# Paged decode: the product of probabilities and latents dealt to four 32-column strips of TensorE

## The chip, the cores and the metric

One core of a Trainium2 chip runs the whole program. The metric is the device time of one execution in microseconds, from the first to the last instruction; it is measured several times, and the median counts.

## What is computed

One inference step of a two-layer trunk. Each layer normalises its input, projects it once to all branch columns, runs a retention branch and a latent-attention branch for 512 prompt tokens and for 8 sequences with 8 new tokens each, and projects back. The change touches only the attention of those 8 sequences over their paged past:

```python
def one(xs):                       # one decode sequence
    pt, qn_s, qp_s, c_s, kpe_s = xs
    c_all = concatenate([cache_ckv[layer, pt].reshape(-1, KV_RANK), c_s])    # 16 pages x 128 rows, and 8 new
    kp_all = concatenate([cache_kpe[layer, pt].reshape(-1, MLA_ROPE), kpe_s])
    kn, v = mla_keys_values(c_all[None], p)          # kn = rmsnorm(c @ w_kb), v = c @ w_vb
    ...
    s = einsum(qn, kn) + einsum(qp, kp_all)
    pr = softmax(where(mask, s * MLA_SCALE, NEG_INF))
    return einsum('bhqk,bkhd->bqhd', pr, v)
```

The kernel never makes v. It computes (pr @ c_all) @ w_vb: the latents (256 wide) are weighted by the probabilities first, and one small product per head follows for all sequences together. All is float32.

## The kernel before, in words

The program is written by hand for five engines with semaphores between them; each engine runs its own list of instructions in the order in which the code stands. A loop of two layers has five stages with a meeting point between them (`stage_end`): the input projection, the latents and prompt keys, retention and prompt attention, the paged decode, and the output projection. The projections are made in three products of rounded high and low parts. The change is in the fourth stage.

In the decode stage the unit is a pair of pages. A sequence has 8 pairs (`PAIRS`), and a layer has 8 sequences. For each pair TensorE turns the next pair's latents (`turn_pair`, L838) and rotary keys (L843), multiplies the turned latents by the key weights with the sequence's queries beside them (`pair_keys`, L861), and multiplies the rotary part (`pair_rotary`, L870). ScalarE keeps the turned latents' high part (L1178), squares the keys (L1191) and keeps the scores (L1194, L1196). VectorE makes the low part (L1547) and sums the squares (L1564), GpSimd takes the inverse root (L1803 to L1810), and VectorE joins the scores (L1573, L1578).

The rest of a sequence, its tail, is spread over the pairs of the next sequence. The functions `sequence` of each engine set the place by the pair's number q: the maximum is turned behind pair 1 (`tail_max_turn`, L878) and spread behind pair 2 (L882), ScalarE takes the exponential behind pair 3 (L1201), and then TensorE does the three steps that the change touches:

- `tail_attend` behind pair 4 (L890): for each of the 16 pages, and for the new rows (`c_new`, 64 rows), the probabilities (128 rows of keys by HQ = 32 columns, 4 heads times 8 queries) are the weights and the page's 256 latents move. All 17 add up in partitions 0 to 31 of one part of PSUM bank 7. After every fourth page a semaphore (`pv_ps`) lets SyncE load four pages of a later sequence into that buffer.
- `tail_den` behind pair 5 (L898): the denominators, which VectorE has summed per partition (L1602), are summed over partitions by a product with one column of ones.
- VectorE divides (`tail_divide`, L1607 and L1609), and `tail_turn` behind pair 6 (L905) turns the 32 x 256 result into two 128 x 32 pieces with a product by the identity. VectorE keeps them (L1616).

The last sequence of a layer has no next one; its tail runs alone at the end of the stage, each step waiting for the last. The closing products with w_vb follow (L946).

```python
                for n in range(KT):
                    ...
                    m = pe.matmul(ps[0:HQ, 7, O_PV:O_PV + KVR], Pr[0:r, b, n, :], rhs,
                                  start=n == 0, stop=n == KT - 1)
```

Page latents and rotary keys come by one DMA each per page, issued by SyncE (L447, L449) after it has read the page number. A table of constants is loaded once at the start (L386).

Of the kernel before, what the change touches and what calls it, by code (L numbers as in the profile page):

```python
# [23 lines left out]
FP32 = mybir.dt.float32  # L24
# [5 lines left out]
P = 128  # L30
# [4 lines left out]
ROPE, QR, KVR = 64, 384, 256  # L35
# [22 lines left out]
QPAGES = NPAGE // QUARTERS  # L58
KT = NPAGE + 1
HQ = H * NT  # L60
LOG_G = np.log1p(-np.exp2(-5.0 - np.arange(H, dtype=np.float32))).astype(np.float32)


def rows(t):
    return ST if t == S_TILE else P
# [3 lines left out]
def constants():  # L69
    f = np.float32  # L70
    p = np.arange(P)
    pos = np.stack([p + P * t for t in range(TILES - 1)] + [NPAGE * PAGE + p % NT], 1).astype(f)

    def rope(dim):
        inv = (f(10000.0) ** (-(np.arange(0, dim, 2, dtype=f) / f(dim)))).astype(f)
        ang = (pos[:, :, None] * inv).astype(f)
        return np.cos(ang).astype(f), np.sin(ang).astype(f)

    cr, sr = rope(DK)
    ca, sa = rope(ROPE)  # L80

    place = np.stack([p, p % NT], 1).astype(np.float64) + 1.0
    g = LOG_G.astype(np.float64)
    dq = np.exp(place[:, :, None] * g)
    dk = np.exp(-place[:, :, None] * g) * DK ** -0.5
    decay = np.concatenate([dq, dk], 2)
    chunk_decay = np.broadcast_to(np.exp(P * g)[None, :], (P, H))
    causal = p[:, None] <= p[None, :]
    future = np.where(p[None, :] <= p[:, None], 0.0, NEG)
    s = np.arange(ST)  # L90
    same = s[:, None] // NT == s[None, :] // NT
    step_mask = np.zeros((P, ST))
    step_mask[:ST] = same & (s[:, None] <= s[None, :])
    new_mask = np.zeros((P, NB, H, NT))
    new_mask[:ST] = np.where(same & (s[:, None] <= s[None, :]), 0.0, NEG).reshape(ST, NB, 1, NT)
    own = np.zeros((P, NB))
    own[:ST] = s[:, None] // NT == np.arange(NB)[None, :]
    parts = [("ident", np.eye(P)), ("ones", np.ones((P, P))), ("causal", causal), ("future", future),
             ("step_mask", step_mask), ("new_mask", new_mask), ("own", own), ("cos_r", cr), ("sin_r", sr),
             ("cos_a", ca), ("sin_a", sa), ("decay", decay), ("chunk_decay", chunk_decay),  # L100
             ("neg_half", np.full((P, 1), -0.5)), ("key_mean", np.tile([[1.0 / DK, EPS]], (P, 1)))]
    at, place_of, cols = 0, {}, []
    for name, a in parts:
        a = np.asarray(a, np.float64).reshape(P, -1).astype(f)
        place_of[name] = (at, a.shape[1])
        cols.append(a)
        at += a.shape[1]
    return np.ascontiguousarray(np.concatenate(cols, 1)), place_of


CONST, PLACE = constants()


def build(nc, x_prompt, x_sample, cache_ckv, cache_kpe, state_ret, page_table, norm_w, w_in, q_a_norm_w,
# [5 lines left out]
    def place(name, shape, dt=FP32, at=base):  # L120
        n = 4 * int(np.prod(shape[1:]))
        tensor = nc.alloc_sbuf_tensor_at(name, shape, dt, offset=at[0])
        at[0] += (n + 31) // 32 * 32
        return tensor
# [4 lines left out]
    def const_view(name):  # L129
        a, n = PLACE[name]  # L130
        return cst[:, a:a + n]

    ident, ones, neg_half = const_view("ident"), const_view("ones"), const_view("neg_half")
    norm_b = place("norm_b", [P, D])
    gn_b = place("gn_b", [P, HW])
    qa_b = place("qa_b", [P, QR])
# [7 lines left out]

    wq_hi = place("wq_hi", [P, KC, HQ + HW + HQ], FP32R)
    wq_lo = place("wq_lo", [P, KC, HQ + HW + HQ], FP32R)
    wvb = place("wvb", [P, KC, HW])
    pages = place("pages", [1, NB * NPAGE], INT32)
    stat = place("stat", [P, 64])
    rstat = place("rstat", [P, 64])  # L150
    pool_tmp = place("pool_tmp", [P, 64])
    A0 = base[0]

    at = [A0]
# [8 lines left out]
    at = [A0]  # L163
# [29 lines left out]
    at = [E0]  # L193
# [26 lines left out]
    at = [D0]  # L220
# [8 lines left out]
    cT_lo = place("cT_lo", [P, 2, 2 * KC, P], FP32R, at)  # L229
    ksq = place("ksq", [P, 2, 2, HQ + HW], FP32, at)  # L230
    kss = place("kss", [P, 2, HALF, H], FP32, at)
    kss_t = place("kss_t", [P, 2, 2, H], FP32, at)
    krs = place("krs", [P, 2, HALF, H], FP32, at)
    nope = place("nope", [P, 2, NPAGE, HQ], FP32, at)
    rot = place("rot", [P, 2, NPAGE, HQ], FP32, at)
    Pr = place("Pr", [P, 2, KT, HQ], FP32, at)
    m1 = place("m1", [P, HQ], FP32, at)
    m2 = place("m2", [HQ, 1], FP32, at)
    mdiag = place("mdiag", [HQ, HQ], FP32, at)
    den = place("den", [P, HQ], FP32, at)  # L240
    rden = place("rden", [HQ, 1], FP32, at)
    on_s = place("on_s", [HQ, KVR], FP32, at)

    N0 = OG[1] - OG[0]
    at[0] = max(at[0], W_HI1)
# [7 lines left out]
    ps = nc.alloc_psum_tensor("ps", [P, 8, 512], FP32)  # L253
# [4 lines left out]
    def sem(name, per_layer=True):  # L258
        s = nc.alloc_semaphore(name)
        if per_layer:  # L260
            layer_sems.append(s)
        return s
# [6 lines left out]
    def mix_tile(k):  # L269
# [45 lines left out]
    den_ok, den_ps, pv_ps, pv_all, on_ok, ot_ps, pv_ok = (sem(n) for n in  # L315
        ("denominators_summed", "denominators_turned", "latents_attended_a_quarter", "latents_attended", "latents_divided",
         "attended_turned", "attended_kept"))
# [207 lines left out]
    def _(pe):  # L525
# [29 lines left out]
        with pe.Fori(0, DEPTH) as L:  # L555
# [36 lines left out]
            for h in range(H):  # L592
                for c in range(KC):
                    n = h * KC + c
                    m = pe.transpose(ps[:, 6 + n // 4, (n % 4) * P:(n % 4 + 1) * P], wkb[:, c, h * DK:(h + 1) * DK],
                                     ident)
# [78 lines left out]
            for c in range(KC):  # L675
                for h in range(H):
                    n = c * H + h
                    m = pe.matmul(ps[:, 0, n * ST:(n + 1) * ST], wkbT[:, h, c * P:(c + 1) * P],
                                  qnT[:, h, SEQ:TOK], start=True, stop=True)
# [194 lines left out]
            O_MT, O_MB, O_PV, O_DEN, O_T = 0, P, P + HQ, P + HQ + KVR, P + HQ + KVR + 1  # L874
# [10 lines left out]
            def tail_attend(s, b):  # L885
                pe.wait_ge(pr_ok, s + 1)
                for n in range(KT):
                    r = ST if n == NPAGE else P
                    rhs = c_new[0:r, :] if n == NPAGE else ckv[b][:, n, :]
                    m = pe.matmul(ps[0:HQ, 7, O_PV:O_PV + KVR], Pr[0:r, b, n, :], rhs,  # L890
                                  start=n == 0, stop=n == KT - 1)
                    if n % QPAGES == QPAGES - 1:
                        m.then_inc(pv_ps, 1)
                m.then_inc(pv_all, 1)

            def tail_den(s):
                pe.wait_ge(den_ok, s + 1)
                pe.matmul(ps[0:HQ, 7, O_DEN:O_DEN + 1], den[:, :], ones[:, 0:1], start=True, stop=True)\  # L898
                    .then_inc(den_ps, 1)

            def tail_turn(s):
                pe.wait_ge(on_ok, s + 1)
                for c in range(KC):
                    o = P + HQ + KVR + 16 + c * HQ
                    m = pe.matmul(ps[:, 7, o:o + HQ], on_s[:, c * P:(c + 1) * P], ident[0:HQ, 0:HQ],  # L905
                                  start=True, stop=True)
                m.then_inc(ot_ps, 1)

            def sequence(seq, b, use, next_use, first, last):
# [27 lines left out]
            tail_max_turn(NB - 1)  # L937
            tail_max_spread(NB - 1)
            tail_attend(NB - 1, 1)
            tail_den(NB - 1)  # L940
            tail_turn(NB - 1)

            pe.wait_ge(pv_ok, NB)
            for h in range(H):
                for c in range(KC):
                    m = pe.matmul(ps[0:ST, 0, h * DK:(h + 1) * DK], olat[:, c, h, :], wvb[:, c, h * DK:(h + 1) * DK],  # L946
                                  start=c == 0, stop=c == KC - 1)
# [30 lines left out]
    def _(act):  # L978
# [11 lines left out]
        with act.Fori(0, DEPTH) as L:  # L990
# [138 lines left out]
            def step_scale(h):  # L1129
                act.wait_ge(up_ok, h + 1)  # L1130
                act.activation(S0[:, h, :, :], S0[:, h, :, :], ACT.Copy, scale=float(np.exp(NT * np.float64(LOG_G[h]))))\
                    .then_inc(up_scaled, 1)
# [117 lines left out]
    def _(dve):  # L1250
# [17 lines left out]
        with dve.Fori(0, DEPTH) as L:  # L1268
# [335 lines left out]

            def tail_divide(s):
                dve.wait_ge(den_ps, s + 1)
                dve.reciprocal(rden[:, :], ps[0:HQ, 7, P + HQ + KVR:P + HQ + KVR + 1])  # L1607
                dve.drain()
                dve.tensor_scalar(on_s[:, :], ps[0:HQ, 7, P + HQ:P + HQ + KVR], rden[:, 0:1], None, ALU.mult)\  # L1609
                    .then_inc(on_ok, 1)  # L1610

            def tail_keep(s):
# [43 lines left out]
            tail_shift(NB - 1, 1)  # L1656
            tail_den(NB - 1, 1)
            tail_divide(NB - 1)
            tail_keep(NB - 1)
            dve.wait_ge(dy_ps, 1)  # L1660
# [20 lines left out]
            for g in range(3):  # L1681
# [3 lines left out]
                for t in range(TILES):  # L1685
                    n = rows(t)
# [161 lines left out]
```

## Time and profile before

| | |
|---|---|
| time, median of 3 runs | 1590.44 us (1587.83, 1592.5, 1590.44) |
| span of the profiled execution, on its one core | 1591.7 us, mean granted TensorE clock 0.936 |
| TensorE busy | 1450.8 us, 91% of the span, 8808 matmul records |
| VectorE, ScalarE, GpSimd busy | 727.7, 520.8, 423.9 us |
| matmul records of the attend (L890) | 544, of which 512 for pages |
| DMA | 115.82 MB, 24.2% of the time of 16 engines on the main queue |

The profiled execution is listed by its span alone, and no time of its own beside it; the span stands 1.3 us above the median of the runs. How to read it: times are microseconds unless marked ns. PE is TensorE's matmul, PEld its weight load, which overlaps PE, DVE VectorE, ACT ScalarE, POOL GpSimd, SP SyncE; a q behind the name is the engine's sequencer. L12 is line 12 of the kernel before. An fp32 product appears as two matmul records with a weight load each. Matmuls are pipelined and their ends are modelled, so the start of a record says more than its length. In the form 128\*32 the first number is the rows of the array that a product uses, the second its columns.

### The profile page before, as it was taken

To read this page: it belongs to the slowest core of one execution; us is meant where nothing else is said; L and a number is where in the kernel's file an instruction comes from. 1 tells how busy PE (TensorE), PEld (TensorE's weight loads), DVE (VectorE), ACT (ScalarE), POOL (GpSimd) and SP (SyncE) were. 2 spreads that over 40 slices of the span, in tenths; PEclk is the share of its full clock that TensorE was granted. 3 is DMA by queue.
4 is the path that set the end of the run, shared out by engine and by line. 5 is a ranking of instruction groups with operands and counts; after the bars stand their busy time and mean duration, and the time that the engine had idled before them with its cause. 6 is when DMAs were issued, how large, how long until landed. Compare 5 with 4: busy or idle time off the path is not lost.

```text
span 1591.7 us, 27121 instructions
## 1 busy us (share of the span) xinstructions
PE 1450.8 (91%) x8808; PEld 1241.1 (78%) x8808; DVE 727.7 (46%) x1366; ACT 520.8 (33%) x1360; POOL 423.9 (27%) x588
## 2 busy tenths in 40 slices
PE   5999987988999999978969999879989999999788
PEld 5999944666988888867959999446569888888578
DVE  4432445375555544543244324463855555545341
ACT  4210234132544444422041112331235444444230
POOL 1000222252544444430010002222525444444200
PEclk9999998588999999988979999975989999999899
DMA  9412020012442222201513210200135222222024
GB/s 307 132 53 74 0 72 0 1 40 70 129 117 67 66 67 66 67 1 59 180 65 127 65 61 0 72 0 1 41 83 165 68 67 66 67 66 67 1 92 166
DMA packets 132774, 115.82 MB, mean 73 GB/s; under 512 B 46513, under 2 KB 127346, under 8 KB 132658
## 3 DMA queue, kind: packets, MB, share of 16 engines
q1 hardware_dynamic: 132658, 114.49, 24.2%
q8 instruction: 46, 0.75, 0.2%
q14 instruction: 70, 0.57, 0.1%
HBM read 103.53 MB, written 13.27 MB: 73 GB/s over the span
## 4 chain that ended last, share of the span: by engine, by line
PE 43%; issue 31%; POOL 14%; POOLq 5%; DVE 4%; ACT 2%; DVEq 1%; DMA 0%; SPq 0%; ACTq 0%
POOL krs L1810 12%; PE ps L529 10%; PE ps L530 10%; PE ps L531 10%; POOL rstat L1703 2%; POOLq L1804 2%; POOLq L1806 2%; PE ps L725 2%; PE ps L890 1%; PE ps L772 1%; PE ps L770 1%; PE ps L543 1%; POOLq L1698 1%; PE ps L735 1%; PE ps L753 1%
## 5 line engine op out<-in xcount | busy, mean ns | idle before, releaser
L529 PE MATMUL ps<-w_hi,hT_hi 128*128 128x408 f32 (+5 forms) x880 | 304.2, 346 | 0.0
L530 PE MATMUL ps<-w_lo,hT_hi 128*128 128x408 f32 (+5 forms) x880 | 302.1, 343 | 0.0
L531 PE MATMUL ps<-w_hi,hT_lo 128*128 128x408 f32 (+5 forms) x880 | 301.2, 342 | 0.0
L1564 DVE TENSOR_REDUCE kss<-ksq 128x8 f32<-128x1024 f32 x128 | 156.0, 1218 | 232.1 <-ACT ksq L1191 232.1
L1191 ACT ACTIVATE ksq<-ps 128x544 f32<-128x544 f32 x256 | 160.0, 625 | 203.3 <-PE ps L861 203.3
L861 PE MATMUL ps<-wq_hi,cT_hi 128*128 128x272 f32 x1024 | 224.5, 301 | 0.0
L1810 POOL TENSOR_TENSOR krs<-kss_t,cst 128x8 f32<-128x8 f32 x128 | 209.1, 1634 | 19.0 <-DVE Ssc L1578 2.5
L861 PE MATMUL ps<-wq_lo,cT_hi 128*128 128x272 f32 x1024 | 213.5, 290 | 0.0
L861 PE MATMUL ps<-wq_hi,cT_lo 128*128 128x272 f32 x1024 | 213.4, 290 | 0.0
L529 PEld LDWEIGHTS ps<-w_hi,hT_hi 128*128 128x128 f32 (+1 forms) x880 | 158.6, 180 | 7.8 <-issue 0.2
L530 PEld LDWEIGHTS ps<-w_lo,hT_hi 128*128 128x128 f32 (+1 forms) x880 | 158.5, 180 | 7.4
L531 PEld LDWEIGHTS ps<-w_hi,hT_lo 128*128 128x128 f32 (+1 forms) x880 | 158.3, 180 | 7.6
L861 PEld LDWEIGHTS ps<-wq_lo,cT_hi 128*128 128x128 f32 x1024 | 162.8, 190 | 0.0
L861 PEld LDWEIGHTS ps<-wq_hi,cT_lo 128*128 128x128 f32 x1024 | 162.7, 190 | 0.0
L861 PEld LDWEIGHTS ps<-wq_hi,cT_hi 128*128 128x128 f32 x1024 | 161.3, 191 | 0.1
L1697 POOL TENSOR_SCALAR pool_tmp<-stat 128x1 f32<-128x1 f32 (+2 forms) x70 | 18.3, 261 | 491.4 <-ACT ps L1025 296.7
L1291 DVE TENSOR_SCALAR z<-ps 128x408 f32 (+3 forms) x80 | 45.7, 579 | 205.9 <-PE ps L531 205.7
L1178 ACT ACTIVATE cT_hi<-ps 128x512 fp32r<-128x512 f32 x128 | 77.6, 606 | 147.1 <-PE ps L838 146.0
L1547 DVE TENSOR_TENSOR cT_lo<-ps,cT_hi 128x512 fp32r<-128x512 f32 x128 | 87.3, 682 | 78.0 <-ACT cT_hi L1178 77.6
L890 PE MATMUL ps<-ckv,Pr 128*32 128x256 f32 x512 | 118.3, 391 | 3.0 <-ACT Pr L1201 3.0
L1803 POOL TENSOR_TENSOR kss_t<-kss,cst 128x8 f32<-128x8 f32 x128 | 29.0, 226 | 338.0 <-DVE kss L1564 338.0
L1005 ACT ACTIVATE w_hi<-raw 128x816 fp32r<-128x816 f32 x64 | 52.0, 877 | 202.8 <-PE ps L531 200.9
(181 smaller groups left out, 1948.1 us busy)
## 6 DMA issues: line engine op xcount, KB each, us to landing
ckv<-in_cache_ckv SPq DMA_DIRECT2D x256, 128.0 KB, 2.1
raw<-in_w_in SPq DMA_DIRECT2D x68, 408.0 KB, 4.4
kp<-in_cache_kpe SPq DMA_DIRECT2D x256, 32.0 KB, 1.8
raw<-in_w_out SPq DMA_DIRECT2D x16, 340.0 KB, 4.0
S<-in_state_ret SPq DMA_DIRECT2D x8, 512.0 KB, 5.9
out<-S SPq DMA_DIRECT2D x8, 512.0 KB, 3.2
z<-out SPq DMA_DIRECT2D x2, 2048.0 KB, 8.7
wqb<-in_w_qb SPq DMA_DIRECT2D x3, 1152.0 KB, 10.1
```

What stands on the lines that cost most here:

```text
L529: pe.matmul(out, a_hi, b_hi, start=first, stop=False)
L530: pe.matmul(out, a_hi, b_lo, start=False, stop=False)
L531: return pe.matmul(out, a_lo, b_hi, start=False, stop=last)
L861: m = pe.matmul(ps[:, 1 + 2 * j + side, 0:CUT], x, w[:, c, w0:w0 + CUT], start=c == 0 and k == 0, stop=c == KC - 1 and k == 2)
L890: m = pe.matmul(ps[0:HQ, 7, O_PV:O_PV + KVR], Pr[0:r, b, n, :], rhs, start=n == 0, stop=n == KT - 1)
L1005: act.activation(w_hi[:, par, 2 * k:2 * k + 2, :], raw[:, k, :, :], ACT.Copy).then_inc(w_hi_ok, 1)
L1178: act.activation(cT_hi[:, par, :, :].rearrange("p a n -> p (a n)"), ps[:, 0, :], ACT.Copy)\
L1191: act.activation(ksq[:, q % 2, j, :].rearrange("p (s c) -> p s c", s=2), ps[:, 1 + 2 * j:3 + 2 * j, 0:CUT], ACT.Square).then_inc(kk_sq, 1)
L1291: dve.tensor_scalar(dst, ps[0:n, t, 0:GW], 1.0, None, ALU.mult).then_inc(z_kept, 1)
L1547: dve.tensor_tensor(cT_lo[:, par, :, :].rearrange("p a n -> p (a n)"), ps[:, 0, :], cT_hi[:, par, :, :].rearrange("p a n -> p (a n)").bitc ...
L1564: dve.tensor_reduce(kss[:, hs, 2 * k:2 * k + 2, :], ksq[:, q % 2, :, c0:c0 + HW].rearrange("p j (h k) -> p j h k", h=H), AX.X, ALU.add).th ...
L1810: pool.tensor_tensor(krs[:, hs, c, :], tmp, spread_col(neg_half[:, 0:1]), ALU.pow)\
```

## The change

The 17 products of the attend are dealt round over four groups of 32 partitions of PSUM, which are four groups of 32 columns of the array: product n goes to strip n modulo 4. Each strip starts its own sum at its first product and ends it at its last, so four partial sums stand in 128 partitions. The denominators are written to all four strips, by four products. VectorE's reciprocal and multiplication work on 128 partitions instead of 32. The turning product adds the four partial sums: its weights are now 128 rows high, and instead of the 32 x 32 identity it takes a new constant of 128 x 32, `fold`, which has a one where the row number modulo 32 is the column number. The number and the order of all other instructions stay as they are, as do all waits. TensorE has three more one-column products per tail. The table of constants grows from 1823 to 1855 columns, and three small buffers for statistics shrink to make room.

```diff
@@ constants
+STRIPS = P // HQ
...
+             ("fold", p[:, None] % HQ == np.arange(HQ)[None, :]),
@@ buffers
-    stat = place("stat", [P, 64])
-    rstat = place("rstat", [P, 64])
-    pool_tmp = place("pool_tmp", [P, 64])
+    stat = place("stat", [P, 40])
+    rstat = place("rstat", [P, 48])
+    pool_tmp = place("pool_tmp", [P, 48])
...
-    rden = place("rden", [HQ, 1], FP32, at)
-    on_s = place("on_s", [HQ, KVR], FP32, at)
+    rden = place("rden", [P, 1], FP32, at)
+    on_s = place("on_s", [P, KVR], FP32, at)
@@ TensorE, tail_attend
-                    m = pe.matmul(ps[0:HQ, 7, O_PV:O_PV + KVR], Pr[0:r, b, n, :], rhs,
-                                  start=n == 0, stop=n == KT - 1)
+                    k = n % STRIPS
+                    m = pe.matmul(ps[k * HQ:(k + 1) * HQ, 7, O_PV:O_PV + KVR], Pr[0:r, b, n, :], rhs,
+                                  start=n < STRIPS, stop=n + STRIPS >= KT)
@@ TensorE, tail_den
-                pe.matmul(ps[0:HQ, 7, O_DEN:O_DEN + 1], den[:, :], ones[:, 0:1], start=True, stop=True)\
-                    .then_inc(den_ps, 1)
+                for k in range(STRIPS):
+                    m = pe.matmul(ps[k * HQ:(k + 1) * HQ, 7, O_DEN:O_DEN + 1], den[:, :], ones[:, 0:1],
+                                  start=True, stop=True)
+                m.then_inc(den_ps, 1)
@@ TensorE, tail_turn
-                    m = pe.matmul(ps[:, 7, o:o + HQ], on_s[:, c * P:(c + 1) * P], ident[0:HQ, 0:HQ],
-                                  start=True, stop=True)
+                    m = pe.matmul(ps[:, 7, o:o + HQ], on_s[:, c * P:(c + 1) * P], fold, start=True, stop=True)
@@ VectorE, tail_divide
-                dve.reciprocal(rden[:, :], ps[0:HQ, 7, P + HQ + KVR:P + HQ + KVR + 1])
+                dve.reciprocal(rden[:, :], ps[:, 7, P + HQ + KVR:P + HQ + KVR + 1])
                 dve.drain()
-                dve.tensor_scalar(on_s[:, :], ps[0:HQ, 7, P + HQ:P + HQ + KVR], rden[:, 0:1], None, ALU.mult)\
+                dve.tensor_scalar(on_s[:, :], ps[:, 7, P + HQ:P + HQ + KVR], rden[:, 0:1], None, ALU.mult)\
                     .then_inc(on_ok, 1)
```

## Rows read from the trace of the kernel before

**Rows 1.** The page's head: span, busy time of each engine.
```profile
span 1591.7 us, 27121 instructions
PE 1450.8 (91%) x8808; PEld 1241.1 (78%) x8808; DVE 727.7 (46%) x1366; ACT 520.8 (33%) x1360; POOL 423.9 (27%) x588
```
**Rows 2.** Stretches: us, busy PE, PEld, DVE, ACT, POOL, granted clock, DMA share, GB/s.
```profile
441.15:448.72 7.57, 7.57 (x35) 3.57 (x34) 3.06 (x4) 0.77 (x3) 2.79 (x4) 1.00 0.70 211
448.72:481.50 32.78, 32.03 (x258) 31.34 (x257) 17.42 (x28) 17.91 (x55) 14.03 (x21) 1.00 0.23 62
```
**Rows 3.** Who waited for whom, 420 to 700: waiter, releaser, total, times, longest.
```profile
PE ps L878 <- DVE m L1585: 3.5, 7, 0.8
PE ps L838 <- DVE cT_lo L1547: 2.2, 7, 0.3
...
SPq L447 <- PE ps L890: 62.6, 6, 12.6
```
**Rows 4.** The line of the attend, L890: duration ns min/median/max, starts, forms.
```profile
L890 PEld LDWEIGHTS ps<-ckv,Pr x512: 106/110/178, 441.2 to 1513.2; 128*32 128x32 f32 x171
L890 PE MATMUL ps<-ckv,Pr x512: 378/379/636, 441.2 to 1513.5; 128*32 128x256 f32 x171
```
**Rows 5.** Timeline of an attend's pages: start us, us long, engine, line, count.
```profile
441.15 0.14 PEld L890 LDWEIGHTS ps<-ckv,Pr 128*32 128x32 f32 x2
...
441.15 6.61 PEld L890 LDWEIGHTS ps<-ckv,Pr 128*32 128x32 f32 x32
441.15 7.09 PE L890 MATMUL ps<-ckv,Pr 128*32 128x256 f32 x32
```
**Rows 6.** Timeline of TensorE, the denominators.
```profile
452.60 0.22 PE L898 MATMUL ps<-cst,den 128*32 128x1 f32 x2
```
**Rows 7.** Timelines of the two tails that end a layer.
```profile
712.83 9.36 PE L890 MATMUL ps<-ckv,Pr 128*32 128x256 f32 x32 [1.50 <-ACT Pr L1201]
713.26 0.18 PEld L890 LDWEIGHTS ps<-ckv,Pr 128*32 128x32 f32 x1 [0.25 <-issue]
...
717.49 4.21 PEld L890 LDWEIGHTS ps<-ckv,Pr 128*32 128x32 f32 x20 [0.22 <-issue]
...
723.16 0.47 DVE L1609 TENSOR_SCALAR on_s<-ps,rden 32x256 f32<-32x256 f32 x1
724.69 1.96 PE L946 MATMUL ps<-wvb,olat 128*64 128x128 f32 x16 [0.38 <-DVE olat L1616]
...
1516.34 3.53 PE L946 MATMUL ps<-wvb,olat 128*64 128x128 f32 x16 [0.38 <-DVE olat L1616]
```
**Rows 8.** Timeline of TensorE from the last page to the next pair.
```profile
447.65 0.59 PE L890 MATMUL ps<-ckv,Pr 128*32 128x256 f32 x2
448.18 0.62 PE L890 MATMUL ps<-c_new,Pr 64*32 64x256 f32 x2
```
**Rows 9.** Timeline of TensorE around the turning product.
```profile
456.37 0.33 PE L870 MATMUL ps<-qp_s,kpT 128*128 x2
456.62 0.52 PEld L905 LDWEIGHTS ps<-cst,on_s 32*128 32x128 f32 x4
457.18 0.65 PE L838 MATMUL ps<-cst,ckv 128*128 128x128 f32 x4
```
**Rows 10.** Timeline of TensorE where a pair follows a pair without a tail.
```profile
460.78 0.33 PE L870 MATMUL ps<-qp_s,kpT 128*128 x2
460.95 0.61 PE L838 MATMUL ps<-cst,ckv 128*128 128x128 f32 x4
```
**Rows 11.** Timeline of VectorE and ScalarE beside and behind the attend.
```profile
443.90 1.08 DVE L1602 TENSOR_REDUCE den<-Pr 128x32 f32<-128x544 f32 x1
...
449.42 0.60 ACT L1178 ACTIVATE cT_hi<-ps 128x512 fp32r<-128x512 f32 x1 [7.50 <-PE ps L838]
```
**Rows 12.** Timeline of SyncE: first issues of the first and third quarter.
```profile
443.25 0.35 SPq L447 DMA_DIRECT2D kp<-in_cache_kpe  x1
...
457.34 0.33 SPq L447 DMA_DIRECT2D kp<-in_cache_kpe  x1
```

More of the change, by code:

```diff
@@ L133, in build @@
     ident, ones, neg_half = const_view("ident"), const_view("ones"), const_view("neg_half")
+    fold = const_view("fold")
     norm_b = place("norm_b", [P, D])
```

## The prediction

> **What bounds the kernel now.** I read the page's head first, then the busy times of two stretches, then who waits for whom, then single lines of TensorE. TensorE is busy for 91% of a span of 1591.7 us, no other engine for half of it [rows 1]. A share over the whole span says nothing of one stage, so I cut out one sequence of the paged decode [rows 2]: the stretch from the end of one attend to the start of the next (448.72 to 481.50) has TensorE busy for 32.03 of 32.78 us, and the attend itself (441.15 to 448.72) for all of its 7.57 us, while VectorE works 3.06, ScalarE 0.77 and GpSimd 2.79 us in it. The granted clock is 1.00 in both, the upper level (2.4 GHz). In 280 us TensorE waits twice per sequence, 0.8 and 0.3 us at most, never around the attend [rows 3]. So inside the decode TensorE's own time is the time, and what the attend loses the kernel gains, as long as nobody else becomes late.
>
> What does the attend consist of? Sixteen pages and the new rows, each a product of 128 (or 64) rows by 32 columns with 256 moving columns. In the trace each fp32 product is two records with a weight load each (two halves): 512 records for 16 tails of 16 pages [rows 4]. In a tail 32 records stand in one row of 7.09 us, each 0.379 long [rows 5]; the last thus begins 6.71 us after the first, so starts are 6.71 / 31 = 0.216 us apart. The record's length is not its cost; the distance of starts is. A product costs 0.432 us and uses 32 of the array's 128 columns. The weight loads' row is 6.61 us long beginning at the same moment: loads run beside the matmul before them. Two loads from 441.15 make a row of 0.14, one takes 0.110 [rows 4, 5], so a load claims about 0.03 us.
>
> **The change, part by part.**
> *Pages on four strips.* The same 17 products in the same order, but neighbours write other partitions and sit in other columns. No row of this trace has two products in different columns, so the price of one product behind another must be bounded: from above 0.432 (no overlap) and even more (a switch that costs), from below 0.108, a quarter, if four run at once. What I take rests on how a product is made: its two halves go to the same strip, so the second can't begin before the first has streamed, 0.216 us. Records start in the order of the program in every stretch I looked at [rows 5, 6, 8 to 10]. So the second half of page n and the first half of page n+1 may run together, but the first half of page n+2 stands behind the second half of page n+1. Steady state: one product each 0.216 us, plus a weight load of 0.027 that now falls between: 0.243. First to last record then takes 15 x 0.243 + 0.24 = 3.88 us instead of 6.71, a gain of 2.83 per tail. Without the load's share (0.216) it is 3.23, with a load and a start together, as the one-column halves of the denominators show them (0.05, [rows 6]), it is 0.269 and the gain 2.44. I take the middle. Fourteen tails lie inside the stream: 14 x 2.83 = 39.6 us.
>
> *The two tails that end a layer* stand alone and cold [rows 7]: there the weight loads start 0.423 apart (713.26 to 717.49 in ten steps), twice the usual, so at the lower clock level, 1.2 GHz; before it TensorE had waited for the chain of the maximum and the exponential. From 717.49 on twenty loads take 4.21 us: the clock has risen 4.66 us after the tail's start. With 0.45 cold and 0.243 warm per product: 10.3 products in 4.66 us, 4.7 left, 6.04 us from first to last record against 8.98 (9.36 less 0.38). Twice 2.94, as the second such tail is much the same: 5.9 us.
>
> *The new rows.* The seventeenth product stays a 64-row one in strip 0, with its 0.1 us of emptying before it [rows 8]: nothing gained or lost.
>
> *Denominators.* One product of one column becomes four. The two records of today start 0.05 us apart [rows 6], so six more cost 0.30 if they can't overlap, 0 if they do: 16 x 0.30 = 4.8 us lost. No engine waits for it but TensorE's own queue.
>
> *Turning product.* Its weights grow from 32 to 128 rows. From the rotary product's first record to the next pair's first transpose 0.81 us pass with it [rows 9] and 0.17 without [rows 10]: it costs 0.64. The four loads (0.111 apart, 0.52 us for four) set its pace, and 32 moving columns hide under them whether they are summed over 32 or 128 rows. What goes is the change from 128 rows to 32 and back. So 4 x 0.11 = 0.44, a gain of 0.20 x 16 = 3.2 us. Were the row switch not the reason, the gain is 0.
>
> *VectorE* divides 128 partitions instead of 32: partitions work side by side, 0.47 us as now [rows 7], under TensorE's next pair in all but two tails. *The constants' load*, once at the start, grows by 1.8%, which I cost at nothing.
>
> Sum: -39.6 - 5.9 + 4.8 - 3.2 = **-43.9 us**. Covers, if TensorE is back 2.8 us earlier: VectorE's last work in the attend ends at 444.98, TensorE's next transposes would start at 445.9 [rows 11]. ScalarE waits 7.50 us for them today. The page loads follow the attend by quarters: eight issues from 443.25 to 447, the third quarter at 457.34 [rows 12], so some 28 us for four quarters in a sequence that shrinks from 40.4 to 37.6 us; that queue waits for TensorE, not the reverse [rows 3, 12]. Nothing new is late. The profiled span of 1591.7 stands 0.1% above the median of the runs, 1590.44; taken from the median: **1546.5 us**. Bounds of this case: 0.216 a product gives 1540 (14 x 0.40 more, and 2 x 0.4 in the cold tails), 0.269 gives 1553.
>
> A page speaks to this directly. The Trainium skill, "TensorE: Matmul & The Clock Gate", section on packing small matmuls, says that matmuls start and end in program order; no row here has the strips on which it would show. The same section states that a weight load overlaps a running matmul only where the row group differs. All four strips use all row groups, so by this rule no strip could be filled under another, and instead of 45.5 us nothing would be gained: this is the no-overlap rival below, 1592. The trace does not bear it out in this form: with the same 128 rows the next load begins 0.03 us after the first, under the matmul [rows 5].
>
> **The rivals.**
> *Whole strips run at once.* If each strip keeps its own line of halves and the order binds only within it, a strip takes 7 x 0.216 and the fourth begins 6 x 0.05 later: 1.81 us for 6.71. Gain 4.90 x 14 = 68.6, in the two cold tails 3.26 us instead of 8.98 (11.4 together), less 1.6 because the first layer's closing products would then be cold as the second's are (3.53 against 1.96 us, [rows 7]): with the other terms 1513.6. For it: nothing in one strip touches another. Against: starts are in program order wherever I look. The packing section's figure, 2.38 times for three column tiles, would be on this side; its products are a single pass each.
>
> *No overlap.* The array takes one moving stream at a time, or fills no strip while another runs (what the weight-load rule above would make of it): the 0.216 stay, the small terms remain, +1.6: 1592.0; with a load of 0.027 laid bare at each change of strip (15 x 16 times, 6.5 us) 1598.5. For it: not one pair of records in this trace overlaps in its streaming.
>
> *Each change of strip empties the array.* Going from 128*32 to 64*32 the start comes 0.32 after the last (448.18, and 447.65 + 0.59 - 0.379 = 447.86) [rows 8] instead of 0.216: 0.10 us of emptying. If a new column group counts as a new shape, 15 changes x 0.10 x 16 = 24 us, three more in each denominator 4.8, with the other terms +30.4: 1620.8. It is slower as soon as an emptying costs more than what the strips overlap, which here is nothing, since an emptied array has nothing to overlap with. Against: that row changes the row count, and a strip has the same shape as its neighbour. The Trainium skill, "TensorEngine Tiling (Array Packing)", key properties, says that only a change of mode drains, not of tile; by that, this rival would not happen, and no row here shows it.
>
> **How the numbers follow.** Half product by half product 0.49; whole strips 0.18; a partial overlap between it and none 0.06; no overlap 0.15; emptying 0.12. A measurement of this kernel can tell some 0.3% (4.8 us) from no change. Faster: 0.49 + 0.18 + 0.06 = 0.73. The no-overlap case is mostly within it (0.12), with loads laid bare slower (0.03): same 0.12, slower 0.15. The time is the likeliest case's, whose own range is 1540 to 1553. It holds half the chance only, so the range takes in whole strips (1513.6, and 1510 if the fourth strip starts sooner) and no overlap (1599): 1510 to 1599.
>
> **What would show it.** Starts of neighbouring page products 0.24 apart with the two halves of one 0.216 apart, and the attend (first page record to next transpose) 4.7 us for 7.57; a sequence period of 37.6 for 40.4. The row of denominators 0.5 long for 0.22, the turning product's stretch 0.6 for 0.81. Four halves starting within 0.2 us would mean whole strips; 0.216 between all records no overlap; 0.32 at each change emptying. A clock under 1.00 in the decode, or TensorE waiting for a page or for VectorE after the attend, would make the sum wrong with its mechanism right.

## The result, and the profile after

| | before | changed kernel |
|---|---|---|
| time, median of 4 runs each | 1591.47 us (1587.83 to 1594.19) | 1507.34 us (1504.36 to 1509.20) |
| ratio | | 0.9469, 95% interval 0.9449 to 0.9488 |
| span of the profiled execution | 1591.7 us | 1503.9 us |
| TensorE busy, records | 1450.8 us, 8808 | 1365.3 us, 8904 |

The change gains 84 us, nearly twice the 43.9 forecast, and lies 2.7 us below the range. The page's head of the changed kernel, against [rows 1]; line numbers are now 3 to 6 higher than before (the attend is L894, the denominators L903, the turning product L911):

```profile
span 1503.9 us, 27313 instructions
PE 1365.3 (91%) x8904; PEld 1199.1 (80%) x8904; DVE 727.1 (48%) x1366; ACT 520.6 (35%) x1360; POOL 424.3 (28%) x588
```

The other engines' busy times stay, and TensorE's falls by 85.5 us. The stretches of one attend and the rest of its sequence (columns as in [rows 2]), and then the decode stages of the two layers:

```profile
440.88:443.29 2.41, 2.41 (x36) 1.07 (x35) 1.74 (x3) 0.77 (x3) 0.86 (x3) 1.00 0.88 307
443.29:475.73 32.44, 31.68 (x264) 31.10 (x264) 18.73 (x30) 17.91 (x55) 15.98 (x23) 1.00 0.31 83
...
385.30:681.40 296.10, 279.05 (x2376) 261.38 (x2377) 164.62 (x258) 149.11 (x456) 134.44 (x192) 0.97 0.30 83
1135.20:1429.60 294.40, 277.37 (x2376) 259.88 (x2376) 164.66 (x258) 149.09 (x456) 134.40 (x192) 0.97 0.30 84
```

An attend takes 2.41 us for 7.57; the clock is 1.00 as before. The stages were 339.3 and 339.9 us, so 88.7 us went there. The rest of the program took 0.9 us more, which is the closing products, below. The timeline of that attend and of the steps behind it, against [rows 5, 6, 8, 9]:

```profile
440.88 1.93 PE L894 MATMUL ps<-ckv,Pr 128*32 128x256 f32 x32
442.74 0.62 PE L894 MATMUL ps<-c_new,Pr 64*32 64x256 f32 x2
443.29 0.33 PE L841 MATMUL ps<-cst,ckv 128*128 128x128 f32 x1
...
447.17 0.24 PE L903 MATMUL ps<-cst,den 128*32 128x1 f32 x8
447.34 0.33 PE L841 MATMUL ps<-cst,ckv 128*128 128x128 f32 x1
...
450.95 0.33 PE L873 MATMUL ps<-qp_s,kpT 128*128 x2
451.06 0.53 PEld L911 LDWEIGHTS ps<-cst,on_s 128*128 128x128 f32 x4
451.54 0.31 PE L841 MATMUL ps<-cst,ckv 128*128 128x128 f32 x1
```

Thirty-two page records, nearly all still 0.379 long, stand in 1.93 us: the last begins 1.55 us after the first, where it was 6.71. How many records run in a short stretch shows the pattern (the windows view of the attend's line alone: us, PE busy and count, PEld busy and count, clock, DMA share, GB/s):

```profile
440.88:440.91 0.03, 0.03 (x4) 0.03 (x5) 1.00 1.00 367
441.11:441.15 0.04, 0.04 (x8) 0.03 (x4) 1.00 1.30 482
```

Four records have begun after 0.03 us. A record does not name its strip. I take these four for the first halves of four products on four strips, because two halves on one strip begin 0.216 apart or more in every stream that is known to stay on one (`before`, `side_only`). Then come four more together. The starts of single records, read from the trace and counted from the first one, in us:

```
changed kernel: 0.00 0.01 0.01 0.02   0.24 0.25 0.25 0.26   0.46 0.46 0.47 0.48   ...   1.54 1.54 1.55 1.56
```

In the program the second half of page 0 stands before the first half of page 1. In the trace it begins 0.23 us later than that, after pages 1, 2 and 3 have all begun. Strips are 0.007 us apart, and each takes 0.216 per half as before. The runs `blocks4` and `new_rows_128`, below, show starts out of the program's order with no need for that inference. Nobody became late for it: TensorE's waits in the decode are those of [rows 3], and SyncE, which issues the page loads, still waits for the attend:

```profile
PE ps L881 <- DVE m L1590: 3.6, 7, 0.8
PE ps L841 <- DVE cT_lo L1552: 2.2, 7, 0.3
...
SPq L450 <- PE ps L894: 31.7, 6, 7.0
```

The cold tail of the first layer, against [rows 7]:

```profile
674.26 3.64 PE L894 MATMUL ps<-ckv,Pr 128*32 128x256 f32 x32 [1.50 <-ACT Pr L1206]
...
677.83 1.06 PE L894 MATMUL ps<-c_new,Pr 64*32 64x256 f32 x2
678.82 0.28 PE L903 MATMUL ps<-cst,den 128*32 128x1 f32 x8
...
681.40 3.67 PE L951 MATMUL ps<-wvb,olat 128*64 128x128 f32 x16 [0.38 <-DVE olat L1621]
```

The attend takes 4.56 us there for 9.84 (first page record to the denominators), all at the lower level, and the closing products run cold too, 3.67 us for 1.96. In the second layer the clock rises at the end of the attend, and the closing products take 2.67 us for 3.53:

```profile
1423.11:1426.68 3.57, 3.57 (x32) 1.36 (x32) 1.08 (x1) 0.00 (x0) 0.00 (x0) 0.50 0.00 0
1429.62:1432.30 2.68, 2.67 (x16) 2.27 (x16) 0.00 (x0) 0.00 (x0) 0.00 (x0) 0.70 0.00 0
```

So the closing products lose 1.7 us in one layer and win 0.9 in the other. That a shorter attend leaves them cold is not shown. `layout_only`, with the attend of the kernel before, has them at 3.62 and 3.58, and `new_rows_128`, with a still shorter attend than here, at 1.96 in both layers. What sets their level stays open.

### The profile page after: what moved, and what is told of

It reads as the page before. It is cut to its first block, busy times and chain, and to the rows that moved or that the text cites. A ratio compares the mean times of both kernels' runs of the same rounds, so it can differ in the third digit from the quotient of the medians.

```text
span 1503.9 us, 27313 instructions
## 1 busy us (share of the span) xinstructions
PE 1365.3 (91%) x8904; PEld 1199.1 (80%) x8904; DVE 727.1 (48%) x1366; ACT 520.6 (35%) x1360; POOL 424.3 (28%) x588
## 4 chain that ended last, share of the span: by engine, by line
PE 46%; issue 27%; POOL 15%; POOLq 6%; DVE 3%; ACT 2%; DVEq 1%; DMA 0%; SPq 0%; ACTq 0%
POOL krs L1815 13%; PE ps L532 11%; PE ps L533 11%; PE ps L534 10%; POOL rstat L1708 2%; POOLq L1809 2%; POOLq L1811 2%; PE ps L728 2%; PE ps L775 1%; PE ps L773 1%; PE ps L738 1%; PE ps L546 1%; PE ps L793 1%; PE ps L784 1%; POOLq L1703 1%
## 5 line engine op out<-in xcount | busy, mean ns | idle before, releaser
L1183 ACT ACTIVATE cT_hi<-ps 128x512 fp32r<-128x512 f32 x128 | 77.6, 606 | 72.2 <-PE ps L841 70.8
L841 PE MATMUL ps<-cst,ckv 128*128 128x128 f32 x512 | 82.8, 285 | 13.6 <-DVE cT_lo L1552 6.9
```

The lines of the kernel that those rows point to most:

```text
L841: m = pe.transpose(ps[:, 0, (2 * j + c) * P:(2 * j + c + 1) * P], ckv[b][:, 2 * q + j, c * P:(c + 1) * P], ident)
L1183: act.activation(cT_hi[:, par, :, :].rearrange("p a n -> p (a n)"), ps[:, 0, :], ACT.Copy)\
```

## The experiments

There are ten runs: eight further kernels, and two of the kernels a second time. Each is compared with runs of the kernel before on its chip. Two theories stood at first. **A**: each strip has its own line of waiting halves. **B**: products start in the program's order, and only halves of one product are passed by the next. **C**, own lines that are short, was the third.

**Blocks of four** (`blocks4`).

```diff
-                    k = n % STRIPS
+                    k = n // 4 % STRIPS
```

Here and in the other kernels with blocks, `start` and `stop` move with it to each strip's first and last product.

> The changed kernel with the sixteen pages dealt in blocks: four neighbours to one strip, then four to the next. Theory A (each strip has its own line of waiting halves, and one strip's line does not hold up the next): nothing changes against the changed kernel, 1507 us give or take 4, first to last page record 1.56 us. Theory B (products start in program order; only the two halves of one product may be passed by the next product): overlap only where a block ends, last record 5.4 us after the first, 3.85 us more per tail, about 1569 us. Theory C (own lines, but short ones: a few waiting records at most can be passed): between the two, with the records showing how many of one strip's products start before the next strip's first.

Measured: 1547.21 us, ratio 0.9727 (0.9699 to 0.9755): neither A (1507) nor B (1569). The attend is 5.07 us:

```profile
440.74:445.81 5.07, 5.07 (x35) 2.52 (x35) 3.06 (x4) 0.77 (x3) 2.79 (x4) 1.00 0.80 262
```

```
strip 0:  0.00 0.24 0.46 0.67 0.89 1.10 1.32 1.54
strip 1:                      0.89 1.13 1.35 1.57 1.78 2.00 2.21 2.43
strip 2:                                          1.79 2.03 ...
strip 3:                                                         2.68 ... 4.22
```

Strip 1 begins 0.006 us after the fifth half of strip 0, when exactly three of strip 0's halves still wait (the sixth to eighth). Strips 2 and 3 repeat it. This is C, and it gives the length of the line: one running and three waiting; a fifth stops everything behind it, other strips' halves too. This kernel also shows the order of starts directly. The record that raises `pv_ps` for the first four pages is the second half of page 3, the eighth page record of the program. In the trace it is the eleventh to start, at 1.54 us: three halves of strip 1 have passed it, the first of them 0.64 us earlier.

**Blocks of two** (`blocks2`; `k = n // 2 % STRIPS`).

> The changed kernel with the pages dealt in pairs: two neighbours to one strip. Theory A (own lines): as the changed kernel, 1507 us, 1.56 us from first to last page record. Theory B (products start in program order): each pair costs one product's 0.432, last record 3.67 us after the first, about 1541 us. Theory C (own but short lines): nearer to the changed kernel than blocks of four.

Measured: 1507.74 us, ratio 0.9473 (0.9449 to 0.9497), the same as the changed kernel; the page records stand in 1.97 us.

```profile
440.57 1.97 PE L894 MATMUL ps<-ckv,Pr 128*32 128x256 f32 x32
```

Two products are four halves and just fill a strip's line. All four strips begin within 0.04 us, with three halves waiting on each. The limit is thus the strip's own: with four strips, nine halves wait when the fourth starts. B is out, as it wanted 1541.

**Two strips** (`strips2`).

```diff
-STRIPS = P // HQ
+STRIPS = 2
...
-                    m = pe.matmul(ps[:, 7, o:o + HQ], on_s[:, c * P:(c + 1) * P], fold, start=True, stop=True)
+                    m = pe.matmul(ps[:, 7, o:o + HQ], on_s[0:STRIPS * HQ, c * P:(c + 1) * P],
+                                  fold[0:STRIPS * HQ, :], start=True, stop=True)
```

> The changed kernel with two strips instead of four (products alternate, denominators twice, the turning product over 64 rows). Theory A: sixteen products in eight rounds of 0.432, first to last page record 3.25 us, 1.69 more than with four strips, about 1533 us. The rule of the prediction (the second half of one beside the first half of the next) gives the same for two strips, since it never used more than two; what it gets wrong should appear only from the third strip on. No overlap at all would be near 1590.

Measured: 1537.69 us, ratio 0.9662 (0.964 to 0.9685).

```profile
438.52 3.65 PE L894 MATMUL ps<-ckv,Pr 128*32 128x256 f32 x32
442.10 0.62 PE L894 MATMUL ps<-c_new,Pr 64*32 64x256 f32 x2
```

From first to last page record 3.65 - 0.38 = 3.27 us, as Theory A had it (3.25). The pace is one product each 0.216, which is also that of the prediction's rule without its load; but the rule puts the first half of page 1 beside the second half of page 0, 15 x 0.216 + 0.24 = 3.48 us from first to last (3.88 with the load). The expectation above calls the two the same, and they are not. In the trace two records have begun after 0.02 us (the windows view of the attend's line alone):

```profile
438.52:438.54 0.02, 0.02 (x2) 0.02 (x2) 1.00 0.00 0
```

So the rule has the order wrong from the second strip on; only its pace still fits two strips, and from the third on that fails too. The time is 5 us over the expected 1533. The turning product is the larger part of it: its weights are 64 rows high here, which is still another row count than its neighbours', and from the rotary product to the next transpose 0.82 us pass as in the kernel before, not 0.59. That is 14 x 0.23 = 3.2 us that the expectation had left out. The two cold tails with their closing products are 5.1 us longer than in the changed kernel, which is more than the 2 us or so that the expectation left for them.

```profile
450.29 0.33 PE L873 MATMUL ps<-qp_s,kpT 128*128 x2
450.56 0.63 PE L911 MATMUL ps<-cst,on_s 64*128 64x32 f32 x4
451.11 0.66 PE L841 MATMUL ps<-cst,ckv 128*128 128x128 f32 x4
```

**Everything but the dealing** (`side_only`; the attend with `k = 0`, start at the first and stop at the last product; it leaves out the other three partial sums, so what the turning product adds up is no attention).

> Everything of the change but the dealing: all seventeen products stay in strip 0, the denominators go to four strips, the division is over 128 partitions and the turning product over 128 rows. Partitions 32 to 127 of the weighted latents hold what an earlier stage left there, so the decode output is no attention. Expected from the trace of the changed kernel: the turning product saves 0.23 us a tail, the denominators cost 0.02, 3.4 us in all: 1588 us, no difference that can be told from the kernel before. If the side parts were worth more than 8 us, the strips would be worth that much less than the 84 us.

Measured: 1586.03 us, ratio 0.9958 (0.9946 to 0.9969): 6.6 us less, where 3.4 was expected and the interval reaches from 5 to 9. Its rows of the denominators and of the turning product:

```profile
449.11 0.24 PE L903 MATMUL ps<-cst,den 128*32 128x1 f32 x8
449.29 0.66 PE L841 MATMUL ps<-cst,ckv 128*128 128x128 f32 x4
...
453.07 0.58 PE L911 MATMUL ps<-cst,on_s 128*128 128x32 f32 x4
453.49 0.63 PE L841 MATMUL ps<-cst,ckv 128*128 128x128 f32 x4
```

The turning product's stretch is 0.23 us shorter than before and the denominators' 0.02 longer, as in the changed kernel. So the side parts carry some 0.4% (0.54% at the interval's end) of the change's 5.3%, and the dealing the rest. The first sequence is 0.34 us shorter here, 0.13 more than these two rows explain. From attend to attend the seven distances of a layer are 0.21 to 0.42 us shorter, 2.2 us together, where the rows explain 1.5.

**The memory alone** (`layout_only`: the new constant is loaded and unused, buffers as in the change, all work as before).

> The kernel before with nothing of the change but its memory: the new constant is loaded and not used, the three small buffers shrink, the two grow, so most tensors of the decode lie at other addresses. With the side parts alone the decode stage came out 2.8 and 3.2 us shorter per layer where the tail's own rows explain 1.7; 0.1 us per sequence of the rest lay in the key products (3.09 for 3.11 us a pair). If addresses do that, those products are at 3.09 here too and the stage is 1 us shorter than in the kernel before (339.3 and 339.9), the time 1 to 3 us lower, too little to be told. If they stay at 3.11, the rest comes with the turning product or the denominators.

Measured: 1595.19 us, ratio 1.0006 (0.9991 to 1.0022): no difference that can be told. One sequence (start of an attend to the next) in this kernel, in `side_only` and in the kernel before:

```profile
438.51:478.76 40.25, 39.49 (x292) 34.80 (x292) 20.46 (x32) 18.68 (x58) 16.84 (x25) 1.00 0.31 88
```
```profile
437.67:477.68 40.01, 39.26 (x298) 34.67 (x298) 20.50 (x32) 18.67 (x58) 16.84 (x25) 1.00 0.32 95
```
```profile
441.15:481.50 40.35, 39.60 (x292) 34.91 (x292) 20.47 (x32) 18.68 (x58) 16.82 (x25) 1.00 0.32 90
```

The first sequence is 0.10 us shorter with the memory alone, in the key products of some pairs (3.05 to 3.09 us for 3.11). It differs by sequence: the seven distances of a layer are up to 0.19 us shorter, 0.6 us together in the first layer and 0.5 in the second. The time does not show it, and in the profiled execution the closing products run at 3.62 and 3.58 us for 1.96 and 3.53. Why other addresses make the key products shorter stays open.

**Blocks of three** (`blocks3`; `k = n // 3 % STRIPS`, the new rows in strip 0), a number forecast from the rule that `blocks4` gave.

> The changed kernel with the pages dealt in blocks of three (0-2 to strip 0, 3-5 to strip 1, 6-8 to 2, 9-11 to 3, 12-14 to 0 again, 15 to 1). The run of blocks of four showed the next strip starting just when three halves of the strip before were still waiting. If that is the rule (a strip holds one running and three waiting halves, and a fifth stops everything behind it), strip 1 starts 0.46 us after strip 0, strip 2 at 0.93, strip 3 at 1.39, page 12 at 1.86, and the last page record starts 2.96 us after the first: 1.40 more than the changed kernel, about 1530 us. If four could wait, strip 1 would start at 0.24 and the last record at 2.4, about 1521. If the limit lay in all waiting halves together and not in one strip, blocks of two would have shown it; nothing here should.

Measured: 1527.09 us, ratio 0.9588 (0.9564 to 0.9612).

```profile
441.53 3.33 PE L894 MATMUL ps<-ckv,Pr 128*32 128x256 f32 x32
444.79 0.62 PE L894 MATMUL ps<-c_new,Pr 64*32 64x256 f32 x2
```

3.33 - 0.38 = 2.95 us from first to last page record, for 2.96 expected; strips 1, 2 and 3 begin at 0.46, 0.92 and 1.39, as expected. Four waiting halves would have given 0.24 and 2.4.

**The new rows over 128 rows** (`new_rows_128`).

```diff
+            dve.memset(c_new[ST:P, :], 0.0)
             dve.tensor_copy(c_new[0:ST, :], zc(S_TILE, C_C, KVR))
...
-                    r = ST if n == NPAGE else P
+                    r = P
```

> The changed kernel with the product of the new rows over 128 rows instead of 64 (64 rows of zeros added, whose probabilities are zero too). If what stands before and behind that product (0.31 us from the last page record to it, and 0.31 from it to the next transpose) is partly the array emptying at a change of shape, the product starts one round, 0.216, after the last page of its strip, and the tail is 0.14 us shorter: 2.2 us in all, 1505. If the gaps have another cause, nothing changes.

Measured: 1501.15 us, ratio 0.9421 (0.9402 to 0.9441).

```profile
440.32 1.93 PE L894 MATMUL ps<-ckv,Pr 128*32 128x256 f32 x32
442.07 0.59 PE L894 MATMUL ps<-c_new,Pr 128*32 128x256 f32 x2
442.60 0.33 PE L841 MATMUL ps<-cst,ckv 128*128 128x128 f32 x1
```

The product starts 1.75 us after the first page record instead of 1.86, and 2.28 us pass until the transposes instead of 2.41: 0.13 per attend, as expected. So the gap ahead of a 64-row product was the change of shape. The cold attends give another 1 us each (3.42 us for 4.56 and 4.40), and the closing products behind them run at the upper level in both layers, 1.96 us for 3.67 and 2.67. These are some 6 us, and so is the distance of the times, 6.2; but the changed kernel's time is from another set of runs, and 2.4 of the 6 are the level of the closing products.

In the cold tails of this kernel the denominators follow the new rows at once, all in the form 128\*32, and the rows of the first one show who passes whom:

```profile
675.88 0.48 PE L894 MATMUL ps<-c_new,Pr 128*32 128x256 f32 x1
675.88 0.28 PE L903 MATMUL ps<-cst,den 128*32 128x1 f32 x6
676.19 0.38 PE L894 MATMUL ps<-c_new,Pr 128*32 128x256 f32 x1
676.41 0.20 PE L903 MATMUL ps<-cst,den 128*32 128x1 f32 x2
676.70 0.17 DVE L1613 RECIPROCAL rden<-ps 128x1 f32<-128x1 f32 x1 [3.16 <-PE ps L903]
```

In the program the two halves of the new rows come first, then eight halves of denominators, strip 0's two ahead of the others. In the trace six of the eight start before the second half of the new rows, and the last two, which are strip 0's, behind it. The last half of the program, strip 3's, carries the signal `den_ps` for VectorE. It starts 0.44 us before the first of strip 0's two. Its signal, though, comes 0.71 us after its start (0.75 in the second layer), where 0.21 is usual: only when strip 0's denominators are done too. So starts pass each other and this signal did not, and one signal on the last product still covered all of them.

**The new rows spread over the strips** (`new_rows_spread`).

```diff
+                w = KVR // STRIPS
+                for k in range(STRIPS):
+                    m = pe.matmul(ps[k * HQ:(k + 1) * HQ, 7, O_PV + k * w:O_PV + (k + 1) * w], Pr[:, b, NPAGE, :],
+                                  c_new[:, k * w:(k + 1) * w], start=False, stop=True)
```

> As the last, and the 256 columns of the new rows dealt over the four strips, 64 to each, added to the strip's own partial sum (the turning product sums them anyway). If strips run side by side, the new rows cost one round of 2 x 0.054 instead of 2 x 0.216 on one strip with three idle: first page record to next transpose about 1.96 us for 2.41, 6.3 us over fourteen tails and some 1.6 in the two cold ones, 1499 us. If pieces of one bank in different strips got in each other's way, it would be no better than with 128 rows alone.

Measured: 1499.10 us, ratio 0.9405 (0.9378 to 0.9432).

```profile
438.25 1.93 PE L892 MATMUL ps<-ckv,Pr 128*32 128x256 f32 x32
440.00 0.29 PE L898 MATMUL ps<-c_new,Pr 128*32 128x64 f32 x8
440.23 0.66 PE L841 MATMUL ps<-cst,ckv 128*128 128x128 f32 x4
```

1.98 us for the attend, as expected. To take its distance from the changed kernel on one chip, both ran again together:

> The changed kernel once more, beside the two others of this call, so that its distance from the spread of the new rows is taken on one chip: 1507 us.

> The spread of the new rows once more. From the stretches of the traces (0.455 us less per attend in the stream, some 1 us in each cold one) it should be 8 to 9 us under the changed kernel: 1498.5. The first comparison gave 8.2 between calls.

Measured: 1505.89 us, ratio 0.9454 (0.9439 to 0.947), and 1499.25 us, ratio 0.9402 (0.9384 to 0.9421). 6.6 us less on one chip, and the intervals do not meet; two executions of one program differ by as much as the 2 us that are missing to the expected 8 to 9. This version beats both kernels, 5.98% under the kernel before. Against the padding alone (`new_rows_128`) it is 2 us less by the medians, and those intervals overlap; the attend's rows, 1.98 for 2.28 us, are what speaks for the spreading.

## Why the prediction was wrong, point by point

*The bound was read rightly.* TensorE was the bound of the decode, and what its attend lost the kernel gained: 14 x 5.16 = 72.2 us in the stream and 5.3 + 5.7 = 11.0 us in the cold tails. Nothing in the stream became late, though TensorE came back 5.2 us earlier and not 2.8.

*The step that failed* is the one on the halves: "the second half of page n and the first half of page n+1 may run together, but the first half of page n+2 stands behind the second half of page n+1". Its ground was that records start in the order of the program. All rows behind it were from one array or one strip, where order and waiting for the same columns can't be told apart. With more strips the starts are out of order: page 3's first half precedes page 0's second by 0.22 us, and with two strips page 1's first half already precedes it, by 0.23. The page part of an attend takes 1.55 us from first to last record for the forecast 3.88. What holds is one line per strip, one running and three waiting (`blocks4`, `blocks3`), and dealing round keeps all four strips busy, with four starts in each round of 0.216. The mechanism was the rival "whole strips run at once", at 0.18. I had its reason right and still gave 0.49 to a rule that no row had tested. The rule of program order that the prediction quotes would not have warned me either: it says the same as mine, and the starts contradict it. So do the loads contradict the rule that a weight load overlaps only a matmul of other rows; eight of them begin within 0.05 us, all on the same rows.

*That rival's size* was off as well, 1513.6 for 1507.3: I let the fourth strip begin 0.30 us late, from the distance of two one-column halves on the same strip [rows 6]. Strips are 0.007 apart, so the attend's page part is 1.55 us and not 1.81, 3.6 us over fourteen tails. The denominators, below, are 4.5 us more. The range's lower end, 1510, is this rival with the fourth strip at once, so what it lacked was the denominators: with both put right the rival comes to 1505.5, and 1507.3 was measured.

*Denominators*: forecast +4.8 us, measured 0.02 us per tail, 0.3 in all. The eight records take 0.24 us for 0.22 of two; the lower bound, 0, was the right end. I had taken them as unable to overlap in the same text that let pages overlap.

*Turning product*: forecast -0.20 us a tail, measured 0.76 to 0.53 (last rotary record to the next transpose), -0.23: right, and for the reason given: with 128 rows the emptying before and behind is gone while its four loads keep their distance, and with 64 rows (`strips2`) the gain is nil.

*Weight loads* do not add 0.027 to a round: loads for other strips go under running matmuls of the same rows, and the round stays 0.216. *The cold tails* gave 11.0 us where the rival had 11.4 and the forecast 5.9; the 1.7 us lost in the cold closing products of the first layer came as that rival had it, but by its reason or by luck is open: `new_rows_128` has them warm behind a shorter attend. *No overlap* and *emptying at each change of strip* are out: the first by the four starts in 0.03 us, the second by the 0.007.

*The sum as measured*, from the two traces: the fourteen tails in the stream give 72.2 + 3.2 (turning) - 0.3 (denominators) + 1.5 (key products) = 76.6 us. The cold tails, from the first page record to the closing products, went from 11.86 and 12.11 us to 7.14 and 6.51, which gives 10.3: 0.7 of the attends' 11.0 went on denominators and turning products. The closing products cost 0.85 net. The starts of the two decode stages give 1.8; 1.5 of it are the first key products of the second layer, whose first 4.03 us had a granted clock of 0.78 for 0.50, and nothing shows that the change did that. Together 87.9, against 87.8 between the two spans; the medians are 84.1 apart.

## What to carry to other kernels

A product with 32 or fewer output columns, repeated and summed, is worth dealing over four column strips when TensorE is the bound: the pages' part fell from 6.71 to 1.55 us, 4.3 times, and the sum over strips was free because a product by the identity had to follow anyway (give that product the row count of its neighbours: with 64 rows its 0.23 us was not won). Deal them round, one or two fp32 products to a strip at a time; here four in a row to one strip cost 40 us of the 84 and three cost 20. Then look at what is left beside the strips: padding a 64-row product to the shape of its neighbours and spreading it over the strips gave another 6.6 us.

## What the runs showed of the hardware that I had not expected

Records of matmuls start out of the program's order when they are on different column strips: by 0.22 us and three products in the changed kernel, by 0.64 us in `blocks4`. The signal of a product was held back until the earlier ones of the program were done (`new_rows_128`: 0.71 and 0.75 us after the record's start, for 0.21 elsewhere). A strip's line held one running and three waiting halves in two kernels built to fill it, and a fifth half held up every later product on all strips. Four strips streamed 256 fp32 columns each at once with no loss: a round is 0.216 us with one, two or four strips. Four partial sums in one PSUM bank, and four quarter-wide additions to them, did not get in each other's way.
